# Moving a small u/v product across a stage seam and spreading key searches between gate products, in a hybrid decoder layer

## The reference, cut to what matters

```python
z = x @ w_in                              # q, k, v, qi, ki, wi, u, vb, ga, gb
sc = index_scores(qi, wi, ki)             # sum over 4 heads of relu(qi . ki) * wi
_, idx = lax.top_k(sc, 256)               # every query keeps 256 keys
attn = sparse_attend(q, k[idx], v[idx], valid)
vn = layer_norm(vb, ln_v_g, ln_v_b)
gm = u * (w_spatial @ vn + b_spatial)     # chunks of 128 positions, 4 groups
merged = sigmoid(ga + b0) * (attn @ w_branch_a) + sigmoid(gb + b1) * (gm @ w_branch_b)
```

## Time and profile before

| what | us |
|---|---|
| median of 3 runs (lowest, highest) | 1551.05 (1545.45, 1553.15) |
| the profiled execution's own time | 1560.32 |
| its span, first to last instruction | 1558.7 |
| TensorE busy in the span | 1439.7 (92%) |
| VectorE busy | 724.5 (46%) |
| ACT, POOL busy | 297.2 (19%), 254.4 (16%) |

### The profile page before, as it was taken

The page is one execution under the profiler, slowest core; times in us unless marked ns, Lnnn a source line. Parts: engine busy times, 40 slices in busy tenths (PEclk is TensorE's granted clock), DMA queues, the critical chain, the costliest instruction groups (busy, mean ns, idle before and its releaser), DMA issues. The chain is left out here.

```text
span 1558.7 us, 17701 instructions
## 1 busy us (share of the span) xinstructions
PE 1439.7 (92%) x5707; PEld 782.1 (50%) x5707; DVE 724.5 (46%) x1639; ACT 297.2 (19%) x656; POOL 254.4 (16%) x308
## 2 busy tenths in 40 slices
PE   7999999799999999898989898999489999999985
PEld 2444444344566666565757564555244444444431
DVE  0201023788888889954648444566411111111125
ACT  0100122221221111102554200000011111111114
POOL 3131000133310000201351000011112111121103
PEclk9999999799999999998999899999689999999998
DMA  9221001400122111101331196111089999989835
GB/s 312 69 65 35 15 15 69 129 0 1 41 95 75 70 61 61 70 19 51 92 92 62 55 345 260 28 37 32 15 334 337 347 342 345 352 337 354 325 125 227
DMA packets 72474, 221.89 MB, mean 142 GB/s; under 512 B 16634, under 2 KB 42234, under 8 KB 62042
## 3 DMA queue, kind: packets, MB, share of 16 engines
q1 hardware_dynamic: 56138, 184.64, 33.0%
q0 software_dynamic: 14992, 35.90, 6.6%
q10 hardware_dynamic: 1280, 0.53, 0.2%
HBM read 190.56 MB, written 38.84 MB: 147 GB/s over the span
## 5 line engine op out<-in xcount | busy, mean ns | idle before, releaser
L1786 PE MATMUL main_ps_experts<-w_gate_up,main_e_rowsT 128*128 128x512 f32 x512 | 227.7, 598 | 1.2 <-DVE main_e_rowsT L1891 1.2
L906 DVE TENSOR_SCALAR_CACHE_REDUCE front<-score,bound 128x384 bf16<-128x384 f32 (+2 forms) x198 | 174.2, 943 | 19.2 <-DVE bound L932 18.9
L234 PE MATMUL ps_front<-front,x_all 128*128 128x512 f32 (+1 forms) x448 | 180.4, 557 | 1.7 <-ACT wi L364 1.7
L1786 PEld LDWEIGHTS main_ps_experts<-w_gate_up,main_e_rowsT 128*128 128x128 f32 x512 | 95.7, 192 | 110.6 <-issue 110.6
L234 PEld LDWEIGHTS ps_front<-front,x_all 128*128 128x128 f32 x448 | 83.2, 190 | 91.7 <-issue 81.2
L1896 DVE TENSOR_TENSOR main_hidden<-main_hidden,main_ps_experts 128x256 f32<-128x256 f32 x32 | 13.5, 421 | 221.1 <-ACT main_hidden L1843 221.1
L1520 PE MATMUL ps_merge<-w_o,mergedT 128*128 128x512 f32 x256 | 113.4, 601 | 3.0 <-DVE h_rows L1651 3.0
L733 PE MATMUL ps_gate<-x_all,w_gate 128*128 128x344 f32 x384 | 116.0, 461 | 0.0
L1813 PE MATMUL main_ps_experts<-w_down,main_hiddenT 128*128 128x512 f32 x256 | 115.3, 593 | 0.5 <-ACT main_hiddenT L1848 0.5
L733 PE MATMUL ps_gate<-x_all,front 128*128 128x344 f32 x384 | 113.2, 453 | 0.0
L733 PEld LDWEIGHTS ps_gate<-x_all,w_gate 128*128 128x128 f32 x384 | 74.3, 194 | 38.9 <-issue 2.4
(11 more groups left out here) (296 smaller groups left out, 1784.0 us busy)
## 6 DMA issues: line engine op xcount, KB each, us to landing
w_gate_up<-in_w_gate_up SPq DMA_DIRECT2D x32, 2048.0 KB, 8.7
w_down<-in_w_down SPq DMA_DIRECT2D x32, 1024.0 KB, 11.9
w_gate_up<-pair_out SPq DMA_DIRECT2D x8, 1024.0 KB, 12.0
front<-in_w_qkvi SPq DMA_DIRECT2D x8, 930.0 KB, 20.0
w_gate<-in_w_gate SPq DMA_DIRECT2D x4, 1280.0 KB, 6.0
front<-in_w_gate SPq DMA_DIRECT2D x4, 1280.0 KB, 5.9
h_rows<-in_x_rows SPq DMA_DIRECT2D x9, 512.0 KB, 6.0
h<-h_rows SPq DMA_DIRECT2D x18, 256.0 KB
```

The costliest lines, as they stand in the source:

```text
L234: mm = nc.tensor.matmul(ps[:, g % 2, 0:c1 - c0], x_all[:, k, t * P:(t + 1) * P], w[:, k, c0:c1], start=(k == 0), stop=(k == KC - 1))
L906: V.tensor_scalar(waste[0:n, at - width:at], s, column(bound, g), None, compare, ALU.add, accum_out=column(number, g)).then_inc(taken, 1)
L1786: mm = nc.tensor.matmul(ps[:, GU, :], rowsT[j][:, k, :], w_gu[jw][:, k, :], start=(k == 0), stop=(k == KC - 1))
```

## The change

Four parts. (1) The sampled tokens' u/v product is made in the front end, its first four chunks before and its last four after the last unit's dots, into bank 0; ACT's last instruction of the front end waits for it. PSUM is one tensor for both stages, so that the gate stage can read it. (2) u has two banks, 6 and 0 in turn. (3) In the last pair the place transposes come before the second product of piece 2, and single seeks between the products of the pieces 3 to 5. In every piece 5 gate a comes last; POOL multiplies before it is done, and its store goes second. (4) The wait for the gate stores moves from the end of the gate stage to the start of attention, on SP, POOL and VectorE.

```diff
@@ front end
+            def make_few_uv(ks):
+                for k in ks:
+                    if k == 0:
+                        pe.wait_ge(early_in, 16 * KC // 2)
+                        pe.wait_ge(acc_read, AFTER_FEW + 5 * (NT - 1) + 4)
+                    if k >= KC // 2:
+                        pe.wait_ge(w_uv_in[k], 16)
+                    for g in range(4):
+                        mm = nc.tensor.matmul(ps[g * FEW:g * FEW + N_SAMPLE, FEW_UV_BANK, 0:QUARTER], x_few[:, k, 0:N_SAMPLE],
+                                              w_uv(k)[:, g * QUARTER:(g + 1) * QUARTER], start=(k == 0), stop=(k == KC - 1))
+                if ks[-1] == KC - 1:
+                    mm.then_inc(few_uv_full, 1)
...
             for n in range(len(units) - 2, len(units)):
                 score_dots(n)
+                make_few_uv(range(0, KC // 2) if n < len(units) - 1 else range(KC // 2, KC))
...
                 rectify(n)
+            act.wait_ge(few_uv_full, 1)
@@ gate stage
-        U, V, MIX, TURN = 0, 1, 2, 3
+        U, V, MIX, TURN = (6, FEW_UV_BANK), 1, 2, 3
+        def products(at):
+            return (1, 2, 0) if at == 5 else (0, 1, 2)
...
-                    for which, name in ((0, "gate_a"), (1, "merged_b")):
+                    for which, name in ((1, "merged_b"), (0, "gate_a")):
+                        if at == 5 and which == 0:
+                            sp.wait_ge(gates_read, (blk - j) * 9 + at * 3 + 9)
...
-            for j in range(2):
-                sp.wait_ge(made_out[j], 32 * KC * 3 // 2)
...
             def make_uv(t):
-                for b in (U, V):
-                    if t >= 1:
-                        pe.wait_ge(uv_read, 2 * t - 1 + b)
+                if t == 1:
+                    pe.wait_ge(few_step, 4)
+                if t >= 2:
+                    pe.wait_ge(uv_read, 2 * t - 3)
+                for half, bank in enumerate((U[t % 2], V)):
+                    if half and t >= 1:
+                        pe.wait_ge(uv_read, 2 * t)
...
-            make_few()
...
-                        for which in range(3):
+                        for which in products(at):
                             if ahead:
                                 ahead(at, which)
...
-                        if between:
-                            between(at)
...
+            seek_at = {(3, 0): 0, (3, 1): 1, (3, 2): 2, (4, 1): 3, (4, 2): 4, (5, 1): 5, (5, 2): 6, (5, 0): 7}
-            def find_rows(at):
-                if at == 1:
+            def find_rows(at, which):
+                if (at, which) == (2, 1):
                     turn_places()
-                for b in ((), (), (0, 1), (2, 3), (4, 5), (6, 7))[at]:
+                if (at, which) in seek_at:
+                    b = seek_at[at, which]
                     pe.wait_ge(hot_ready, b + 1)
...
-            make_gates(KC // 2 - 1, between=find_rows)
+            make_gates(KC // 2 - 1, ahead=find_rows)
...
-                        pool.wait_ge(gates_read, i * 18 + at * 3 + 9)
+                        pool.wait_ge(gates_read, i * 18 + at * 3 + (8 if at == 5 else 9))
@@ attention
+        def wait_for_gates_stored(eng):
+            for j in range(2):
+                eng.wait_ge(keep["made_out"][j], 32 * KC * 3 // 2)
...
         def _(sp):
+            wait_for_gates_stored(sp)
             sp.dma_start(first[:], ins["first_masks"]).then_inc(const_in, 16)
             sp.dma_start(own_b[:], ins["rank"][:, 0:N_SAMPLE]).then_inc(own_in, 16)
...
+            wait_for_gates_stored(pool)
             for b in range(N_SAMPLE):
                 pool.wait_ge(masked, 2 * b + 1)
...
+            wait_for_gates_stored(dve)
             step(nc.vector.memset(own_row[:], 1 << 20))
```

More of the change, by code:

```diff
@@ L615, in choose_keys_and_gate @@
         multiplied = sem("multiplied")
-        made_out = [sem(f"made_out{j}") for j in range(2)]
+        made_out = keep["made_out"]
         chunk_out = sem("chunk_out")
@@ L719, in last_mix, with make_gates @@
                     pe.wait_ge(gm_read, TILES)
-            def make_gates(i, ahead=None, between=None):
+            def make_gates(i, ahead=None):
                 for j in range(2):
@@ L725, in make_gates @@
                         at = j * 3 + p
-                        for which in range(3):
+                        for which in products(at):
                             if ahead:
                                 ahead(at, which)
-                            pe.wait_ge(gates_read, i * 18 + at * 3 + which + 1)
+                            pe.wait_ge(gates_read, i * 18 + at * 3 + products((at + 4) % 6).index(which) + 1)
                             chunks = KC if which < 2 else GROUPS
@@ L786, in read_uv @@
                 t, j = i - 1, i % 2
-                act.wait_ge(uv_full, 2 * t + 2)
+                act.wait_ge(uv_full, 2 * t + 1)
                 if i >= 2:
                     act.wait_ge(gm_turned, i - 1)
-                nc.scalar.copy(u[j][:], ps[:, U, :]).then_inc(uv_read, 1)
-                act.wait_ge(uv_full, 2 * t + 3)
+                nc.scalar.copy(u[j][:], ps[:, U[t % 2], :]).then_inc(uv_read, 1)
+                act.wait_ge(uv_full, 2 * t + 2)
                 if i == 2:
@@ L840, in _ @@
                         act.wait_ge(made_out[at % 2], i * 96 + at // 2 * 32)
-                        for which in range(3):
-                            wait_alone(act, gates_full, i * 18 + at * 3 + which + 1, idle[1])
+                        for no, which in enumerate(products(at)):
+                            wait_alone(act, gates_full, i * 18 + at * 3 + no + 1, idle[1])
                             src, to = ps[:, SETS[at % 2][which], 0:n], made[at % 2][:, which, 0:n]
@@ L2155, in build @@
                 keep["w_uv"] = w_uv
+                keep["made_out"] = [whole.enter_context(nc.semaphore(f"made_out{j}")) for j in range(2)]
                 project_and_score(nc, ins, outs, keep)
```

27 lines of the change are left out of this document (11 added, 16 removed).

## The result

The changed kernel's median is **1536.03 us** (nine runs, 1535.0 to 1543.13), against 1545.64 for the kernel before (nine runs, 1541.09 to 1553.61, the three of the forecast among them): a ratio of **0.9933, 95% interval 0.9909 to 0.9957**. The forecast was 1542.0 against a median of 1551.05, which is a ratio of 0.9942.

A forecast was written before the change was run, and what follows sets the result against it. VectorE's key search was taken to bound the stretch up to 662 us, TensorE behind it. An earlier search (1.7), less work behind the places (5.4) and a shorter seam (2.0) gave 9.0 us off 1551.05: 1542.0 us, range 1536 to 1549.

The forecast's parts named there:

- The bound: Gate stage: VectorE's key search is the longer path up to 662 us; TensorE's 4.7 us wait grows to about 8.
- TensorE stays the bound: Rival, chance 0.06: at the place transposes all TensorE's gains would add, 20 us, for a time of about 1531.
- the start gives nothing: Rival, chance 0.18: at the front end's last dots, search starts 0 to 1.5 us later; time 1543.8 to 1545.3.
- the base of the time: Whole kernel: the 9.0 us gain was taken from the median of 1551.05, giving 1542.0 us.
- Part 1: Front end's last dots: half the sampled product fills TensorE's gap, the clock holds, and the search starts 1.7 us sooner.
- Part 2: u/v loop: a second bank for u saves TensorE 4.4 us of waits and VectorE nothing.
- The search: Key search's tail beside POOL's gate products: no change, bounds +0.5 us for a fifth piece, −2 if none.
- Part 3: Gate stage behind the places: TensorE's work falls from 57.6 to 52.2 us, 49.5 at full clock plus 2.7 low clock.
- Part 4: Seam to attention: stores awaited later, logits at low clock ready at +6.1 us, first masks 6.2 us after TensorE's end.
- The sum: Start of attention: first masks at 719.1 us instead of 728.12, 9.0 us earlier, with what lies behind unchanged.
- Stores stand in attention's way: Rival, chance 0.08: at attention's start the last store issues or lands late; gain about 7.5 us, time 1543.5.
- The clock stays low behind the longer wait: Rival, chance 0.04: behind the places TensorE stays at 0.50, 46.8 us more than the sum; time 1589.

The follow-up runs named there:

- e1: Changed kernel with one bank for u again: median 1540.47 us, ratio 0.996 to the kernel before; first masks 475.63 us after the key store, against 475.61.
- e4: Changed kernel with one bit round more in VectorE's key search: median 1549.98 us, first masks 8.0 us later.
- e5: Changed kernel with two bit rounds less in VectorE's key search: median 1527.33 us, first masks 12.5 us earlier.
- e16: The kernel before, unchanged, profiled a second time: 1544.31 us in one execution, 485.77 us from key store to first masks.
- e3: Changed kernel with both halves of the sampled tile's product behind the last dots: median 1539.34 us, ratio 0.9948 to the kernel before.
- e12: Changed kernel with GpSimd's gate-stage products on one column instead of 512 or 344: search 357.65 us instead of 368.1.
- e11: Changed kernel with the sampled tile's product back at the head of the gate stage and one bank for u: median 1540.08 us, ratio 0.9953 to the kernel before.
- e6: Changed kernel with place transposes one product earlier and seeks in pairs, the last pair behind the last product: median 1545.04 us, ratio 0.9984 to the kernel before.
- e8: Changed kernel with the place transposes two products later, seeks moved along: median 1530.61 us, ratio 0.9876 to the kernel before.
- e13: Changed kernel with place transposes three products later, single seeks, the eighth inside the last product: median 1528.57 us, ratio 0.9870 to the kernel before.

## Why the prediction was right or wrong

**The bound: right.** "VectorE's search is the longer path up to 662 us" and "a gain of TensorE ahead of 662 us is worth nothing by itself" are what e1, e4 and e5 show. The wait that should grow to about 8 us grew to 8.98. The rival "TensorE stays the bound" is out, and so is "the start gives nothing".

**The step that failed: the base of the time.** "Against the median 1542.0" takes the gain from a median of three runs, 1551.05. Nine runs of the same kernel, these three among them, have 1545.64, and longer series 1545.99 to 1549.23. This base is 5.4 of the 6.0 us by which the time came out below 1542.0; the gain itself, 9.6 us between the medians instead of 9.0, is the other 0.6. "1560.32 − 9.0 = 1551.3 there" missed because 12 us of that one execution were stalls in attention that a second profile (e16) does not have. The ratio forecast, 0.9942, lies inside the measured interval, 0.9909 to 0.9957.

**Part 1: right in mechanism and size.** The clock held through the filled gap: 1.7 us forecast, 1.86 and 1.39 in the two pairs of traces; e3 shows that it is the gap.

**Part 2: right**, nothing on the path. TensorE itself gained 5.98 us from it, not 4.4: the six waits listed were not its whole cost.

**The search: a term put at nothing.** "I change nothing; bounds +0.5 for a fifth, −2 if none" looked for GpSimd only behind the search, at its multiplies of the last pieces. The tail was indeed as long as before (48.5 us from L959 to L973). But GpSimd delays the bit rounds too, beside the u/v loop and the gates behind it: 8.3 of the 10.5 us that it costs the search (e12), and 1.3 of them went by luck of phase. The group L925 of the kernel before (mean 320 ns for an operation of 171) held the sign of it.

**Part 3: 4.24 instead of 5.4.** Two small misses of one sign: the work behind the places is 50.13 us at the full clock (e5, e11, e12), not 49.5, and the low clock costs 3.2, not 2.7.

**Part 4: 3.09 instead of 2.0.** The step said that TensorE's logits take 3.71 us at the low clock and are ready at +6.1. They took 1.99 at the full clock; what holds the masks is then the load behind SyncE's wait, at +5.1. The step took the low clock for given. That it did not come is not explained by the shorter pause (2.18 us instead of 4.35): behind the same pause the logits took 2.76 us in e5 and 3.63 in e11, and 3.79 behind 1.78 us in e6. Its cause stays open.

**The sum.** 9.0 forecast, 10.5 and 9.9 between the marks of the two pairs of traces. Its terms missed by +1.3 (search), −1.2 (part 3), +1.1 (part 4) and +0.2 us (part 1), so that part of the nearness is luck.

**The other rivals.** "Stores stand in attention's way": a load behind them does set the start, but earlier than the logits did. "The clock stays low behind the longer wait": 1.00 from 665 to 711 us, with the single seeks between the products. The Trainium skill (TensorE: Matmul & The Clock Gate, HAM oscillation) tells of a loop whose every burst of matmuls starts at the low clock behind a wait. Here the wait for the places cost one such start (7.37 us for a product of 4.87), and the bursts behind it stayed at 1.00.

## What to carry to other kernels

Where two engines meet at one instruction, first find which comes later: what the other saves is idle time there, until the meeting point is moved behind work that needs none of it (0.0 and 1.35 us became 5.2 and 6.0). A pause of TensorE can cost a slow start on top of itself: filling the wait from 9 to 2 us gained the time filled (e8) and won back no clock, closing it gave that too (e13). And hang a forecast of half a per cent on a ratio, or on marks around the change, not on a median of three runs.

## What the hardware did that I had not expected

- Behind the wait for the places the slow start hardly depended on the wait's length. For waits of 3.00, 4.37, 8.98, 10.23 and 17.62 us, the same work behind the places took 53.36, 52.77, 53.33, 52.67 and 52.47 us, and 50.13 without a wait: 2.3 to 3.2 us each time. Behind 2.16 us a product of 4.8 took 7.74, and behind only 0.95 us one of 4.87 took 6.57. Not every pause did this: behind 2.2 us at the seam the logits took 1.99 us in twelve traces, 2.76 in e5 and 3.63 in e11.
- Operations of VectorE on seven integers per partition, 0.17 to 0.23 us by themselves, took up to 1.2 us beside GpSimd's products; the passes a hundred times as wide beside the same products took no longer.
- Unchanged code behind the change differed by 12 us between two profiles of one kernel (157.8 and 145.7 us in attention).
